# A hybrid encoder layer on one core: order of the branch units, places of the gates, queues of three kinds of loads

## What is computed

```
xn   = RMSNorm(x);  p = xn @ w_in          # B_a, C_a, x_a | q k v | z | beta, alpha | gate_a | gate_b
u    = conv3_causal(C_a * x_a)             # width-3 depthwise convolution, three taps
y_a  = (B_a * u) @ w_a_out                 # branch A
o    = gated delta rule(silu(conv4(q, k, v)), beta, g), normed, * silu(z)
y_b  = o @ w_b_out                         # branch B
h    = x + (sigmoid(gate_a) * y_a + sigmoid(gate_b) * y_b) @ w_o
y    = h + relu(RMSNorm(h) @ w_up)^2 @ w_down;   out = RMSNorm(y)
```

## Time and profile before

| | us |
|---|---|
| median of three executions | 1772.68 (1766.5 to 1775.85) |
| the profiled execution | 1767.42 |
| its span, first to last instruction | 1765.6 |
| TensorE (PE) busy | 1676.6, 95% |
| VectorE (DVE) busy | 1224.0, 69% |
| ScalarE (ACT) busy | 688.5, 39% |
| GpSimd (POOL) busy | 435.0, 25% |
| HBM traffic | 152 GB/s over the span |

### The profile page before, as it was taken

The page is one execution under the profiler, slowest core; times in us unless marked ns, Lnnn a source line. Parts: engine busy times, 40 slices in busy tenths (PEclk is TensorE's granted clock), DMA queues, the critical chain, the costliest instruction groups (busy, mean ns, idle before and its releaser), DMA issues.

```text
span 1765.6 us, 25674 instructions
## 1 busy us (share of the span) xinstructions
PE 1676.6 (95%) x10233; PEld 1569.3 (89%) x10233; DVE 1224.0 (69%) x1624; ACT 688.5 (39%) x1240; POOL 435.0 (25%) x437
## 2 busy tenths in 40 slices
PE   6998999999989999996949999999999999999998
PEld 6998998999989999996948888888899899999997
DVE  5688646675555857544615288899988977777886
ACT  5122324554333222341202255554454544544444
POOL 1342013434055767553750020000003000000001
PEclk9999999999999999998979999999999999999999
DMA  6121112001767667779566035555564545555543
GB/s 193 43 69 57 48 45 62 1 2 31 239 209 236 199 224 241 246 237 347 190 239 214 1 108 168 179 188 182 184 194 124 166 156 164 159 166 169 167 153 121
DMA packets 212722, 270.18 MB, mean 153 GB/s; under 512 B 9946, under 2 KB 168871, under 8 KB 212604
## 3 DMA queue, kind: packets, MB, share of 16 engines
q1 hardware_dynamic: 170424, 194.57, 35.5%
q10 hardware_dynamic: 32900, 39.36, 6.7%
q0 software_dynamic: 9280, 34.61, 4.9%
HBM read 212.47 MB, written 56.04 MB: 152 GB/s over the span
## 4 chain that ended last, share of the span: by engine, by line
PE 56%; DMA 16%; POOL 8%; DVE 4%; issue 2%; ACT 1%; SPq 1%; POOLq 0%; DVEq 0%; ACTq 0%
PE ps L3433 19%; PE ps L3462 18%; DMA ff_sums<-ff_prep 7%; PE ps L3374 6%; DMA ff_prep<-in_w_up 4%; DMA ff_prep<-in_w_down 4%; PE ps L2450 3%; PE ps L3445 2%; PE ps L1435 2%; PE ps L1458 1%; POOL ff_prep L1995 1%; POOL ff_prep L1999 1%; POOL ff_prep L1997 1%; POOL ff_prep L1993 1%; POOL ff_prep L1988 1%
## 5 line engine op out<-in xcount | busy, mean ns | idle before, releaser
L3075 DVE TENSOR_TENSOR w_lo<-ff_raw,w_hi 128x1024 fp32r<-128x1024 f32 x225 | 276.3, 1234 | 70.8 <-ACT w_hi L2859 70.8
L2859 ACT CAST w_hi<-ff_raw 128x1024 fp32r<-128x1024 f32 x225 | 233.6, 1050 | 161.1 <-PE ps L3462 123.8
L3433 PE MATMUL ps<-x_half,w_hi 128*128 128x320 f32 (+1 forms) x832 | 194.0, 303 | 0.5 <-ACT hid L2896 0.5
L2450 PE MATMUL ps<-xn_hi,g_hi 128*128 128x384 f32 x464 | 158.3, 341 | 4.6 <-DVE b_sb L2287 4.5
L2450 PE MATMUL ps<-xn_hi,g_lo 128*128 128x384 f32 x464 | 156.7, 338 | 0.0
L2450 PE MATMUL ps<-xn_lo,g_hi 128*128 128x384 f32 x464 | 156.6, 338 | 0.0
L3433 PE MATMUL ps<-x_half,w_lo 128*128 128x320 f32 (+1 forms) x512 | 154.9, 302 | 0.0
L3433 PEld LDWEIGHTS ps<-x_half,w_hi 128*128 128x128 f32 x832 | 142.2, 189 | 1.8 <-issue 0.9
L1919 DVE TENSOR_TENSOR g_lo<-g_raw,g_hi 128x512 fp32r<-128x512 f32 x91 | 77.7, 860 | 92.1 <-ACT g_hi L1914 91.7
L3183 DVE TENSOR_TENSOR rows<-ps,rows 128x512 f32<-128x512 f32 x210 | 136.4, 684 | 2.6 <-PE ps L3462 1.8
L707 PE MATMUL ps<-xn_hi,w_hi 128*128 128x384 f32 x312 | 107.9, 346 | 10.5 <-DVE w_lo L836 10.5
(11 more groups left out here) (394 smaller groups left out, 4325.4 us busy)
## 6 DMA issues: line engine op xcount, KB each, us to landing
ff_raw<-ff_sums SPq DMA_DIRECT2D x120, 512.0 KB, 3.7
ff_sums<-ff_prep POOLq DMA_DIRECT2D x60, 512.0 KB, 3.8
ff_raw<-in_w_down SPq DMA_DIRECT2D x57, 512.0 KB, 4.3
ff_raw<-in_w_up SPq DMA_DIRECT2D x48, 512.0 KB, 3.7
ff_prep<-in_w_up SPq DMA_DIRECT2D x32, 512.0 KB, 4.1
ff_prep<-in_w_down SPq DMA_DIRECT2D x56, 256.0 KB, 3.4
g_raw<-in_w_in ACTq DMA_DIRECT2D x22, 512.0 KB, 6.5
gates<-gate ACTq DMA_DIRECT2D x16, 576.0 KB, 7.3
```

What stands on the lines that cost most here:

```text
L2450: last = nc.tensor.matmul(out, a[:, w_of(c)], x(c), start=(start and n == 0 and m == 0), stop=(stop and n == len(ks) - 1 and m == 2), skip ...
L2859: nc.scalar.copy(hi[slot(t, j)][:, :], raw_of(t, j)).then_inc(hi_done, 1)
L3075: nc.vector.tensor_tensor(lo[s][:, :], raw_of(t, j), hi[s][:, :].bitcast(F32), ALU.subtract).then_inc(lo_done, 1)
L3433: last = nc.tensor.matmul(ps[:, PROD_BANK[i] + m, 0:w], y[s][:, at], x[g][i][:, k], start=(NEW[i] and k == 0 and n == 0), stop=(k == 3 and ...
```

## The change

Five things are moved; no arithmetic is.

1. GpSimd's 20 row sums: each of the first twelve waits for its own tile's output, the last eight for slices of z. The three buffers lie elsewhere, so that tile 10's output no longer waits for them.
2. The fourth row sum's load goes from SyncE's queue to ScalarE's, behind the tanh of slice (1, 1), and its cast and rest go some places later.
3. In B pairs the first tap and the tail copies go from VectorE to ScalarE.
4. Branch B's four units come ahead of branch A's. All gates of A, and B's from the fifth on, are loaded to the place of the rounded rows `xn_hi`, which is free after the middle stage.
5. The eight loads of `w_o` go from SyncE's queue to ScalarE's, from unit 4 on, each next to its cast, with other buffers.

```diff
                 def summed(out, x, y, op):
-                    if made[0] % 3 == 0:
-                        pool.wait_ge(out_done, 2 * (made[0] // 3 + 1))
+                    if made[0] < TQ:
+                        pool.wait_ge(out_done, 2 * made[0] + 2)
+                    else:
+                        pool.wait_ge(z_evac, made[0] - TQ + 1)
...
-                    if tile == 10:
-                        dve.wait_ge(sum_a_out, 64)
-                        dve.wait_ge(sum_b_out, 32)
...
-        Y_UNITS = [("yb", 0), ("yb", 1), ("ya", 0), ("ya", 1), ("yb", 2), ("ya", 2), ("yb", 3), ("ya", 3)]
+        Y_UNITS = [(kind, i) for kind in ("yb", "ya") for i in range(4)]
...
-            sp.wait_ge(step_done, 2 * NT - 1)
-            load_sum(sp, 3)
             for n in range(SETS):
                 prep_load(sp, n)
-            closing.sync_first(sp)
             sp.wait_ge(tails_stored, 32)
             closing.sync(sp)
...
+            def first_taps(p):
+                i = PAIRS[p][1]
+                act.wait_ge(hist, 2 * i + 2)
+                act.wait_ge(cleared, 2 * i + 2)
+                act.wait_ge(dve_evac, dve_count[p, "V1s"])
+                for m in range(2):
+                    nc.scalar.activation(acc[m][:, 0:A], pre[m][:, 0:A], ACT.Copy, scale=tap(2 * i + m, 0)).then_inc(tapped, 1)
...
             first_gate(1, 1)
+            load_sum(nc.scalar, 3)
             first_gate(1, 2)
...
                 split(act, p, "S4")
-                if p == 1:
-                    sum_split(3)
...
                 keep(p, 1)
+                if p == 1:
+                    sum_split(3)
...
             act.wait_ge(step_done, PHASE)
-            act.wait_ge(ya_out, YA_OUT + 16 * TA)
-            for f in range(TA):
-                nc.scalar.dma_start(ya_val[f], self.ya_store[f]).then_inc(ya_in, 16)
-            split_y(act, 1)
-            load_gates(act, "ga", 0)
-            load_gates(act, "ga", 1)
+            load_gates(act, "gb", 2)
+            load_gates(act, "gb", 3)
             for i in range(NY):
...
+                if i == 0:
+                    s, base = gate_out[1]
+                    act.wait_ge(s, base + 32 * 4)
+                    act.wait_ge(ya_out, YA_OUT + 16 * TA)
+                    for f in range(TA):
+                        nc.scalar.dma_start(ya_val[f], self.ya_store[f]).then_inc(ya_in, 16)
+                if i == 1:
+                    load_gates(act, "ga", 0)
+                    load_gates(act, "ga", 1)
+                if i == 2:
+                    for f in range(TA):
+                        y_split("ya", f)
...
-        def load_wo(sp, n):
+        def load_wo(act, n):
             if n >= 4:
-                sp.wait_ge(lo_done, n - 3)
+                act.wait_ge(lo_done, n - 3)
             elif n >= 2:
-                sp.wait_ge(self.mid.step_done, self.mid.y6_done)
+                act.wait_ge(self.mid.lo_done, self.mid.y_lots[n + 4])
             else:
-                sp.wait_ge(self.mid.lo_done, self.mid.y_lots[n])
+                act.wait_ge(self.mid.step_done, self.mid.y_done[3])
...
-            for n in range(2, 5):
-                load_wo(sp, n)
             for moved, count in self.sums_stored:
                 sp.wait_ge(moved, count)
             sp.dma_start(gain2[:, :], norm2_g.to_broadcast([P, D])).then_inc(gain_in, 16)
-            for n in range(5, NU):
-                load_wo(sp, n)
             sp.wait_ge(mix_lo, KD)
             for r in (0, 1, 2, 3, 7, 8):
                 load_x(r)
```

More of the change, by code:

```diff
@@ L266, in front @@
         self.x_sums = nc.dram_tensor("x_sums", [4, P, 4, NW], F32).ap()
-        sum_a, sum_b, sum_c = [self.at(f"x_sum{n}", [P, 2, NW], F32, tile_at(10) + n * 3072) for n in range(3)]
+        sum_a, sum_b, sum_c = [self.at(f"x_sum{n}", [P, 2, NW], F32, h + 22016 + n * 3072) for n in range(3)]
         kept = (unit_done, z_tanh, z_evac, *z_out)
@@ L532, in _ @@
                 pool.wait_ge(sum_b_out, 32)
+                pool.wait_ge(sum_c_out, 32)
             @block.vector
@@ L1820, in middle, with tap @@
         rows_of = lambda g: slice(g * NW, (g + 1) * NW)
+        def tap(f, w):
+            return self.vec[:, V_CA + w * TA + f:V_CA + w * TA + f + 1]
         def streams(buf):
@@ L2116, in final, with tails_kept @@
                 (nc.scalar.copy(out, x) if PAIRS[p][0] == "C" else tanh(out, x)).then_inc(act_evac, 1)
+            def first_taps(p):
[5 more added lines that the diff above has]
+                    nc.scalar.activation(acc[m][:, 0:A], pre[m][:, 0:A], ACT.Copy, scale=tap(2 * i + m, 0)).then_inc(tapped, 1)
+            def tails_kept(p):
+                i = PAIRS[p][1]
+                for m in range(2):
+                    nc.scalar.copy(tail[:, 2 * i + m, 0:2], pre[m][:, ROWS_P:ROWS_P + 2]).then_inc(tapped, 1)
+                    nc.scalar.copy(tail[:, 2 * i + m, 2:18].rearrange("p (s t) -> p s t", t=2),
+                                   streams(pre[m])[:, :, SLEN:SLEN + 2]).then_inc(tapped, 1)
             def joined_tanh(p, name):
@@ L2161, in scalar @@
                 last, more = p == NP - 1, p + 1 < NP
+                if PAIRS[p][0] == "B":
+                    first_taps(p - 1)
+                    tails_kept(p - 1)
                 keep(p, 0)
@@ L2319, in convolve @@
                 f = 2 * i + m
[L2320 to L2324 removed]
+                dve.wait_ge(tapped, TAPPED + 6 * i + m + 1)
                 for w in range(1, 3):
[L2326 to L2327 removed]
+                    if w > 1:
+                        dve.wait_ge(conv, 2 * f + 1)
+                    nc.vector.scalar_tensor_tensor(acc[m][:, 0:A], pre[m][:, w:w + A], tap(f, w), acc[m][:, 0:A],
                                                    ALU.mult, ALU.add).then_inc(conv, 1)
[L2329 to L2331 removed]
             def y_rest(kind, f):
@@ L2394, in vector @@
                 rest(dve, p, "A22")
+                if p == 1:
+                    sum_rest(3)
                 if more:
@@ L2425, in vector @@
                     rest_y(dve, i + 2)
-                if i == 1:
+                if i == 3:
                     for f in range(TA):
                         y_rest("ya", f)
+                if i == 5:
+                    closing.vector_split(dve, 0)
                 if i == 6:
+                    closing.vector_split(dve, 1)
+                    closing.vector_mix(dve, range(2, 4))
+                if i == 7:
                     closing.vector_mix(dve, range(4, 6))
-                    closing.vector_split(dve, range(1))
+                    closing.vector_split(dve, 3)
+                merge(i, 0)
+                if i == 6:
+                    closing.vector_split(dve, 2)
                 if i == 7:
-                    closing.vector_split(dve, range(1, 2))
-                merge(i, 0)
-                if i == 7:
-                    closing.vector_split(dve, range(2, 4))
-                    closing.vector_mix(dve, range(6, 7))
+                    closing.vector_split(dve, 4)
                 merge(i, 1)
                 if i == 4:
-                    closing.vector_mix(dve, range(4))
-            closing.vector_split(dve, range(4, 6))
+                    closing.vector_mix(dve, range(2))
+            closing.vector_split(dve, 5)
+            closing.vector_mix(dve, range(6, 7))
+            closing.vector_split(dve, 6)
             closing.vector_mix(dve, range(7, 8))
-            closing.vector_split(dve, range(6, 8))
+            closing.vector_split(dve, 7)
             closing.vector(dve)
@@ L3061, in rest_mix @@
                                            ALU.mult, ALU.subtract).then_inc(mix_lo, 1)
-        def vector_split(dve, ns):
-            for n in ns:
-                rest_wo(dve, n)
         def vector_mix(dve, fs):
```

123 lines of the change are left out of this document (52 added, 71 removed).

## The result

The changed kernel takes 1743.62 us at the median of 4 runs (1743.47 to 1746.95). The kernel before, run beside it, takes 1770.96 (4 runs, 1766.50 to 1775.85). The ratio is 0.985, with a 95% interval of 0.9819 to 0.988: faster by 27 us. The prediction was 1743, with 1728 to 1761 as its range.

A forecast was written before the change was run, and what follows sets the result against it. TensorE, busy 95%, was taken to bound the kernel through its idle stretches, then SyncE's queue of lots. Front -11, lots' start -3.5, traffic +5 put the last sum at 916.8; 26.8 us gained, median 1743, range 1728 to 1761.

The forecast's parts named there:

- What bounds the kernel, and what is late next: TensorE's idle stretches bound it; next, w_o row 2 waits about 30 us for x, queued behind the last of 60 sums.
- The branch gains: Gains of 4, 7 and 38 us on TensorE, said to go into the new wait at row 2.
- Row sums: First block: waiting tile by tile gains 11.5 us, bounds 6 and 14; barrier 0.7 us after TensorE, net 11.
- Fourth row sum: TensorE's 5.9 us gap shrinks to 1 to 3, another of up to 3 can come: gain 4, bounds 0 and 8.
- the start of the lots: SyncE issues the first prepared lot at about 476, not 483: 3.5 us of the 7 taken, bounds 1 and 7.
- Traffic: 5.1 MB of gates and w_o beside the lots at 2.2 us per MB: +11, net +5 us, bounds 0 and +12.
- Gain and x: Behind the last sum, at 916.8: x 5 us from the gain's issue (4 to 7), row 2 starts at 923.3.
- Branch units: Middle stage's end: reordered units and gates leave a 4 us wait before unit 4 (0 to 12); about 38 of 44 back.
- The front gives nothing: Rival: VectorE stays the bound in the first block, everything 11 us later, 1754; chance 0.14.
- No wait for x: Rival: lots run faster, TensorE itself is the bound from 892 on, median 1710; chance 0.07.
- It needs the last sum by 886: Condition set for the rival without a wait for x: last sum 31 us before the forecast's sum.
- Slower: Rival: ScalarE serves w_o loads one at a time, row 2 at 964, 1785; decides from 59 us of delay; chance 0.03.

The follow-up runs named there:

- taps_undone: The changed kernel with the first taps and kept tails of the B pairs back on VectorE: 1745.46 us, 1.8 above the changed kernel.
- x_by_lot_55: Changed kernel with x, gain and roots of rows 0 to 3 moved among the lots, last row sums one z slice sooner: 1706.30 us, again 1703.66.
- last_sum_sooner: The changed kernel with each of the last eight row sums waiting for one slice of z fewer: 1744.42 us.
- x_by_lot_55_taps: x_by_lot_55 with the first taps and kept tails of the B pairs back on VectorE: 1710.17 us, again 1708.14.
- row_sums_only: The kernel before with only the row sums' part of the change: 1758.81 us, ratio 0.9932.

## Why the prediction was right, point by point

**What bounds the kernel, and what is late next: right.** The new wait is where it was put, on the engine it was put down to, behind the transfer that was named: 32.7 us forecast as about 30 (923.3 less 892). TensorE reached row 2 at 893.3. The branch gains went into it; taps_undone shows it for the first taps' part. No run took back the order of the units or the `w_o` loads by themselves; that their 38 us are there shows in TensorE's arrival at 893.3, and in x_by_lot_55, where nothing holds TensorE at row 2.

**Row sums: right in kind, low by 5 us and high by 3.** I took 11.5 of the 16.5 us lost, with 14 as the upper bound; all 16.5 came back. The step that failed is tile 7 after the decay gates, for which I kept 3 us of waiting. I had costed these small instructions as they stood before, beside GpSimd. VectorE's timeline, before and after, at seven of them, and between the two GpSimd's, before:

```profile
126.26 5.34 DVE L658 SCALAR_TENSOR_TENSOR poly<-poly,s 128x36 f32<-128x36 f32 x7
```

```profile
126.60 1.86 POOL L499 TENSOR_TENSOR x_sum<-xn_hi,x_sum 128x768 f32<-128x768 f32 x1
128.54 1.85 POOL L499 TENSOR_TENSOR x_sum<-x_sum,xn_lo 128x768 f32<-128x768 f32 x1
```

```profile
115.30 1.59 DVE L658 SCALAR_TENSOR_TENSOR poly<-poly,s 128x36 f32<-128x36 f32 x7
```

They were stretched by 3.75 us, and GpSimd's two sums beside them, 126.60 to 130.39, lasted 3.79. The change takes those away too. On the other side, I let one sum run behind the last slice but one. In truth VectorE writes three slices of z at once at 219.85, which releases three sums together, and the slices for the last two are there before GpSimd comes to them, so that five sums run back to back:

```profile
220.49 1.84 POOL L501 TENSOR_TENSOR x_sum<-xn_hi,x_sum 128x768 f32<-128x768 f32 x1 [6.41 <-DVE z_sb L309]
...
228.99 1.84 POOL L501 TENSOR_TENSOR x_sum<-x_sum,x_sum 128x768 f32<-128x768 f32 x1
231.12 0.56 POOL L532 DMA_DIRECT2D x_sums<-x_sum  x1 [0.30 <-POOL x_sum L501]
```

The last store is issued at 231.1, lands 4.1 us later, at 235.2, and the barrier opens 2.1 us after that; before, it opened 1.7 us after TensorE's last matmul. So the barrier costs 3.9 us more than before and not 0.7. Net 12.6 for my 11: two misses of opposite sign, and that they partly cancel is luck.

The rule of the Trainium skill that I weighed (SBUF — State Buffer, "Who interferes with whom") says that the loser blocks for the whole instruction. Here the trace agrees with it more than I had allowed: the seven small instructions lost what GpSimd was busy, and a first tap issued 0.1 us behind one sum took its time plus nearly the sum's (timelines of VectorE and GpSimd):

```profile
128.54 2.37 DVE L578 TENSOR_SCALAR acc<-pre,vec 128x1176 f32<-128x1176 f32 x1
```

```profile
128.44 1.83 POOL L501 TENSOR_TENSOR x_sum<-xn_hi,x_sum 128x768 f32<-128x768 f32 x1 [12.80 <-DVE qkv L593]
```

That is 1.54 us more than the 0.83 of the earlier trace rows. I had spread 4.54 us over three sums, and so had 1.5 to 1.7 for one: the same number, by a looser reading. TensorE had the slack for it either way. In the earlier trace rows both engines lose: GpSimd's three sums took 6.97 us there, and 5.5 at the 1.84 that one takes alone.

**Fourth row sum: its second term too small.** The gap of 5.9 us at the third sum step is gone, where I had 1 to 3 left of it. The other one that I had named, of up to 3 us, came: 3.5 us at 482.4, behind the weights' rests that VectorE makes after the sum's rest (475.50 to 477.26). So 2.4 us came back, for my 4. For the start of the lots I took 3.5 us of 7. The first store in the changed kernel is 14.4 us earlier than before, 1.8 beyond the front, which seemed to bear me out or less; but undoing the part costs 6.5 at the medians. A first lot's start is a poor measure of a chain of 60.

**Traffic: the price right, the place wrong.** From first store to last landing the lots took 430.4 us before (495.91 to 926.3) and 435.8 after (481.56 to 917.4): +5.4 for my +5. To half a microsecond that is luck: the last store of last_sum_sooner is 5.1 us away from the changed kernel's, with the same barrier time. But I had put it all in the branch stage. The stores of lot 33, GpSimd's timeline, before and after:

```profile
720.68 0.57 POOL L2001 DMA_DIRECT2D ff_sums<-ff_prep  x1 [0.30 <-POOL ff_prep L1999]
```

```profile
718.28 0.57 POOL L2003 DMA_DIRECT2D ff_sums<-ff_prep  x1 [0.30 <-POOL ff_prep L2001]
```

A lead of 14.4 us has shrunk to 2.4 here, before a single branch unit has run. From here the lots take 196.2 us to their last store where they took 198.0, and that store lands in 3.0 us where it took 7.6. So the sum is made of two misses: the middle stage cost 12 us that I had at nothing, and the branch stage cost some 11 less than I had. In taps_undone the same store is at 711.47 with a barrier 2.6 us later, a lead of 11.8: with the taps on VectorE, the middle stage keeps most of the lead, and it goes later. The other kernels with that edit say the same: lot 33 is stored at 702.76 and 705.30 in the two traces of x_by_lot_55_taps, and at 713.67 and 713.89 in those of x_by_lot_55. So it is the move of the taps that costs the lots their lead in the middle stage. By what it does so is open: TensorE's faster pairs bring their own loads forward, into the lots, but no run varied that by itself.

**Gain and x.** The gain is issued at 917.45 (916.8 forecast). x took 7.1 us from there to VectorE's add, at the bound and not the 5 I chose: two us late. The first row behind the wait took 2.0 us longer than a row at full clock (12.94 against 10.9), as forecast from the earlier trace rows; TensorE had stood idle 32.7 us, and the low level of its clock shows in those matmuls: 14 start in the first 5 us, at a granted clock of 0.62, and 23 in the next 5, at 1.00.

**The sum.** Row 2 began at 926.0 for 923.3, and the span is 1741.5 for 1738.8, the same 2.7. The gain is issued within 0.7 us of the forecast because the terms' misses cancel: the front gave 1.6 more than its term, the lots' first store 1.7 less, the traffic took 0.4 more. The mechanism is what was right; a hit this close is luck. The median agrees with the forecast better than the span does only because the median of before lies above its profiled execution, and that of after on it.

**Branch units.** The wait before unit 4 is 5.1 us for my 4; unit 0 begins at 763.6 where it began at 786.0, 22.4 earlier, for my 11 + 4 + 7. Of these 22.4 the front has 12.6 and the fourth sum 2.4, which leaves 7.4 for the first taps.

**The rivals.** "The front gives nothing" fell with row_sums_only. "No wait for x" was priced right as a state (1710) and rightly given little; x_by_lot_55 reaches 1705 by taking x, gain and roots out of the queue, 3 us of it from the sooner sums. "It needs the last sum by 886" holds only while x, gain and roots stand behind that sum: x_by_lot_55 has no wait for x with its last sum stored at 922.8. "Slower" did not come: the eight `w_o` loads were issued from 822.4 to 866.3, the last rest of their weights begins at 880.6, and TensorE ran through rows 0 and 1 without a wait. Its threshold was wrong, though: with x expected at 923.3, a delay of 31 us of the loads would have set row 2, and 59 is where the kernel becomes slower than before.

## What to carry to other kernels

When an engine's queue paces a stream (here 60 lots on SyncE and GpSimd), list everything that stands behind it in order on each of its engines, small arithmetic included, before costing a move: taking out one leaves the next as the wait, and x, the gain, a root and the last rows of x came out here one after the other. Gains off that queue only lengthen the wait at its end; gains that start it sooner pass through nearly whole (12.0 us at the end for 12.5 at the barrier, 6.5 for 6.8 at the first load), and the price of traffic (2.3 us per MB beside it, 2.2 to 3.1 inside it) decides what may be loaded meanwhile. A stretch beside another engine must be taken out of every instruction in that stretch, the small ones as well.

## What the runs showed of the hardware

- Instructions of VectorE with 36 elements took 0.76 us each beside GpSimd's sums and 0.23 without (5.34 and 1.59 for seven). They lost 3.75 us, and GpSimd was busy for 3.71 beside them.
- The barrier between blocks waits for a store that GpSimd issues: issued at 231.12 beside the last store of z, landed 4.1 us later (the median of its x_sums stores was 2.6 us before), and TensorE's next matmul at 237.41, 2.2 us after the landing.
- 4.2 MB from HBM to HBM on ScalarE's queue delayed the last store of a paced chain of loads and stores on two other queues by 9.6 us (9.0 counted from the first block's barrier), although TensorE did the same work.
- Executions differ by 1.5 to 2.9 us in when GpSimd makes the first sum (64.6 to 65.3, or 66.8 to 67.6), and the first block's barrier moves with it.
